# Five pairs of weight tiles in seven-product form in the input products of both feed-forward networks

## The reference

```python
D_MODEL, SEQ, D_FF = 2048, 256, 5504

def swiglu_ffn(x, w_in, w_out):
    gate, up = jnp.split(x @ w_in, 2, axis=-1)      # w_in: 2048 x 11008
    return (jax.nn.silu(gate) * up) @ w_out

x = x + 0.5 * swiglu_ffn(rmsnorm(x, ffn1_norm), ffn1_w_in, ffn1_w_out)
...
x = x + 0.5 * swiglu_ffn(rmsnorm(x, ffn2_norm), ffn2_w_in, ffn2_w_out)
```

## Time and profile before

| | us |
|---|---|
| median of 3 runs | 1764.4 (1764.1 to 1764.69) |
| the profiled execution, its own time | 1763.82 |
| its span, first to last instruction | 1762.0 |

### The profile page before, as it was taken

The page is one execution under the profiler, slowest core; times in us unless marked ns, Lnnn a source line. Parts: engine busy times, 40 slices in busy tenths (PEclk is TensorE's granted clock), DMA queues, the critical chain, the costliest instruction groups (busy, mean ns, idle before and its releaser), DMA issues.

```text
span 1762.0 us, 20916 instructions
## 1 busy us (share of the span) xinstructions
PE 1755.3 (100%) x8036; PEld 1463.3 (83%) x8036; DVE 1408.5 (80%) x1587; ACT 1074.9 (61%) x1359; POOL 62.7 (4%) x74
## 2 busy tenths in 40 slices
PE   9999999999999999999999999999999999999999
PEld 7788888888988888888888888888888888988887
DVE  7888888887899998575655655888888888799998
ACT  7566666666666666554545544666666666666665
POOL 0000000000000001100000000000000000000000
PEclk9999999999999999999999999999999999999999
DMA  9888788876654556555455547687788887764762
GB/s 378 272 261 260 251 250 249 252 252 201 217 215 184 210 215 208 178 193 177 160 188 163 173 168 262 169 256 244 249 260 260 260 261 240 226 204 166 259 213 90
DMA packets 160691, 391.75 MB, mean 222 GB/s; under 512 B 6504, under 2 KB 15232, under 8 KB 155856
## 3 DMA queue, kind: packets, MB, share of 16 engines
q1 hardware_dynamic: 152288, 342.02, 54.7%
q0 software_dynamic: 7184, 46.42, 12.6%
q10 hardware_dynamic: 1120, 1.97, 0.3%
HBM read 347.37 MB, written 3.69 MB: 199 GB/s over the span
## 4 chain that ended last, share of the span: by engine, by line
PE 95%; DVE 2%; DMA 1%; SPq 1%; issue 1%; ACT 0%; POOL 0%; ACTq 0%; POOLq 0%; DVEq 0%
PE bank L584 9%; PE bank L582 9%; PE bank L583 9%; PE bank L566 7%; PE bank L568 7%; PE bank L567 7%; PE bank L523 7%; PE bank L525 7%; PE bank L524 6%; PE bank L653 5%; PE bank L655 5%; PE bank L654 5%; PE bank L679 3%; PE bank L681 3%; PE bank L680 3%; PE bank L551 1%
## 5 line engine op out<-in xcount | busy, mean ns | idle before, releaser
L1188 DVE TENSOR_TENSOR wlo<-raw,whi 128x1024 fp32r<-128x1024 f32 (+1 forms) x586 | 696.6, 1207 | 224.7 <-ACT whi L849 222.0
L849 ACT ACTIVATE whi<-raw 128x1024 fp32r<-128x1024 f32 (+1 forms) x586 | 611.0, 1047 | 390.2 <-PE bank L525 189.2
L582 PE MATMUL bank<-whi,xs 128*128 128x512 f32 (+1 forms) x768 | 297.9, 388 | 0.4 <-DVE xs L1370 0.2
L584 PE MATMUL bank<-whi,xs 128*128 128x512 f32 (+1 forms) x768 | 295.6, 385 | 0.0
L583 PE MATMUL bank<-wlo,xs 128*128 128x512 f32 (+1 forms) x768 | 295.5, 385 | 0.0
L1188 DVE TENSOR_TENSOR wlo<-tsum,whi 128x1024 fp32r<-128x1024 f32 (+1 forms) x120 | 140.2, 1196 | 60.5 <-ACT whi L849 60.5
L849 ACT ACTIVATE whi<-tsum 128x1024 fp32r<-128x1024 f32 (+1 forms) x120 | 122.2, 1036 | 103.9 <-PE bank L584 64.1
L582 PEld LDWEIGHTS bank<-whi,xs 128*128 128x128 f32 x768 | 144.4, 188 | 29.0 <-issue 0.9
L584 PEld LDWEIGHTS bank<-whi,xs 128*128 128x128 f32 x768 | 144.3, 188 | 27.7
L583 PEld LDWEIGHTS bank<-wlo,xs 128*128 128x128 f32 x768 | 144.4, 188 | 26.8
L653 PE MATMUL bank<-whi,aw_hi 128*128 128x512 f32 x420 | 164.0, 391 | 0.0
(11 more groups left out here) (203 smaller groups left out, 2670.4 us busy)
## 6 DMA issues: line engine op xcount, KB each, us to landing
raw<-ffn_w_in SPq DMA_DIRECT2D x158, 1024.0 KB, 7.1
raw<-ffn_w_out SPq DMA_DIRECT2D x84, 1024.0 KB, 6.5
raw<-w_in SPq DMA_DIRECT2D x48, 1024.0 KB, 5.1
tsum<-raw POOLq DMA_DIRECT2D x36, 1024.0 KB, 7.2
raw<-w_out SPq DMA_DIRECT2D x16, 1024.0 KB, 4.9
raw<-ffn_w_in SPq DMA_DIRECT2D x16, 768.0 KB, 4.6
tsum<-raw POOLq DMA_DIRECT2D x4, 768.0 KB, 5.7
x<-x SPq DMA_DIRECT2D x4, 512.0 KB, 12.4
```

The lines of the kernel that those rows point to most:

```text
L582: mm(banks[b][:, 0:w], xs[:, k + i, 0, tok], hi, start=starts[b] and k + i == 0, stop=False, skip_group_check=True)
L584: last = mm(banks[b][:, 0:w], xs[:, k + i, 1, tok], hi, start=False, stop=k + i == last_k, skip_group_check=True)
L849: A(whi[:, h % SLOTS, 0:n_el], src, ACT.Copy).then_inc(weights_hi, 1)
L1188: V.tensor_tensor(wlo[:, h % SLOTS, 0:n_el], src, whi[:, h % SLOTS, 0:n_el].bitcast(f32), ALU.subtract).then_inc(weights_lo, 1)
```

## The change

The form now takes five pairs of tiles, k = 6 to 10 with k = 11 to 15. Each of the seven products has five tiles, in three halves of two, two and one tile ("mini" half, 512 numbers). The plain tiles are k = 0 to 5: three gate halves GA, GB, GC and three up halves UA, UB, UC. Raw pieces of five tiles go in two DMAs, four tiles into `raw` (five slots) and one into `minis`. The plain pieces are of two tiles, in three slots of their own. `minis`, `tmini` and `last_plain` take the place of `x` in SBUF during the units. So `x` is read again from DRAM behind each network's units (`x_again`), and ahead of the second network POOL first writes it there (`x_kept`). The ring of `whi` and `wlo` keeps four slots.

```diff
-T1, B11, G0, T2, B21, T3, G1, B22, T4, U0, U1 = 0, 2, 4, 6, 8, 10, 12, 14, 16, 18, 20
-UNIT_HALVES = 22
+FORM_K0, FORM_PAIRS = 6, 5
+T1, B11, GA, GB, T2, B21, T3, GC, B22, T4, UA, UB, UC = 0, 3, 6, 7, 8, 11, 14, 17, 18, 21, 24, 25, 26
+UNIT_HALVES = 27
...
+        place[0] = x_at
+        last_plain = sb("last_plain", [P, 2 * W])
+        minis = sb("minis", [P, FORM_SLOTS, W])
+        tmini = sb("tmini", [P, W])
...
             def form(h, bank_out, stationary, w, start):
-                for i in range(2):
+                for i in range(3):
                     pe.wait_ge(weights_lo, h + i + 1)
                     slot = (h + i) % SLOTS
-                    for k in range(2):
+                    for k in range(2 if i < 2 else 1):
...
+            def form_piece(u, j, name):
...
+                wait_free(n)
+                sp.dma_start(raw[:, raw_slot(n), 0:4 * w].rearrange("p (k f) -> p k f", k=4),
+                             w_in[:, k:k + 4, col:col + w]).then_inc(raw_full[raw_slot(n)], 16)
+                if j == 1 and name == "B11":
+                    sp.wait_ge(ss_done, 8 * (2 * u + 1))
+                    if u:
+                        sp.wait_ge(x_psum, 8)
+                        sp.wait_ge(x_stored, 16)
+                sp.dma_start(minis[:, raw_slot(n), 0:w], w_in[:, k + 4, col:col + w]).then_inc(raw_full[raw_slot(n)], 16)
...
             def add_piece(u, j, name, after, done):
...
+                pool.wait_ge(weights_lo, unit_half(u, j) + after + 3)
+                pool.wait_ge(raw_full[raw_slot(n)], RAW_FULL[n])
+                pool.dma_start(tsum[:, 0:4 * w], raw[:, raw_slot(n), 0:4 * w], accum_op=ALU.add).then_inc(done, 16)
+                pool.dma_start(tmini[:, 0:w], minis[:, raw_slot(n), 0:w], accum_op=ALU.add).then_inc(done, 16)
...
             x_power(2)
+            pool.wait_ge(x_updated, 8 * 2)
+            pool.dma_start(x_kept.rearrange("(b p) d -> p b d", p=P), x[:]).then_inc(x_stored, 16)
...
+                for i in range(3):
+                    form_split(T1, i)
+                form_split(B11, 0, "B11")
                 swiglu(u, j - 1)
-                split(base + B11 + 1, piece_half(n + LOAD["B11"], 1, w2), w2)
-                split(base + G0, piece_half(n + LOAD["G0"], 0, w2), w2)
-                split(base + G0 + 1, piece_half(n + LOAD["G0"], 1, w2), w2)
+                for i in range(1, 3):
+                    form_split(B11, i, "B11")
+                plain_split("GA", GA)
+                plain_split("GB", GB)
...
-                split(base + U0 + 1, piece_half(n + LOAD["U0"], 1, w2), w2)
-                split(base + U1, piece_half(n + LOAD["U1"], 0, w2), w2)
+                plain_split("UA", UA)
                 if j + 1 < UNITS:
                     sum_t1(u, j + 1)
-                split(base + U1 + 1, piece_half(n + LOAD["U1"], 1, w2), w2)
+                plain_split("UB", UB)
+                plain_split("UC", UC)
                 if j + 1 < UNITS:
                     sum_t3(u, j + 1)
```

More of the change, by code:

```diff
@@ L166, in sb @@
             return t
+        x_at = place[0]
         x = sb("x", [P, TB, D_MODEL])
+        x_end = place[0]
         xs_at = place[0]
@@ L362, in free, with wait_free @@
                 return weights_lo, QKV + 2 * (n - QKV_P) + 2
+            def wait_free(n):
+                slot = raw_slot(n)
+                shared = {RAW_SLOTS - 1: (RAW_SLOTS - 1, RAW_SLOTS, RAW_SLOTS + 1), RAW_SLOTS: (RAW_SLOTS - 1, RAW_SLOTS),
+                          RAW_SLOTS + 1: (RAW_SLOTS - 1, RAW_SLOTS + 1)}.get(slot, (slot,))
+                for t in shared:
+                    before = [m for m in range(n) if raw_slot(m) == t]
+                    if before:
+                        sem_free, value = free(before[-1])
+                        sp.wait_ge(sem_free, value)
@@ L995, in unit @@
-                act_e.wait_ge(weights_used, base + B11 + 2)
+                plain_split("GB", GB)
+                act_e.wait_ge(weights_used, base + B11 + 3)
                 act_e.wait_ge(act_f_done, 2 * (UNITS * u + j))
                 A(p1s[:, 0:w], Y[:, 0:w], ACT.Copy).then_inc(copied, 1)
-                act_e.wait_ge(t2_added, 16 * (first + 1))
-                for i in range(2):
-                    split(base + T2 + i, tsum[:, i * w2:(i + 1) * w2], w2)
-                loaded(n + LOAD["B21"])
@@ L1002, in unit @@
-                for i in range(2):
-                    split(base + B21 + i, piece_half(n + LOAD["B21"], i, w2), w2)
+                act_e.wait_ge(t2_added, 32 * (first + 1))
+                for i in range(3):
+                    form_split(T2, i)
+                loaded(unit_piece(u, j, "B21"))
+                for i in range(3):
+                    form_split(B21, i, "B21")
                 act_e.wait_ge(sums_done, 2 * first + 2)
-                split(base + T3, piece_half(n + LOAD["B12"], 0, w2), w2)
@@ L1006, in unit @@
-                act_e.wait_ge(weights_used, base + T2 + 2)
+                form_split(T3, 0, "B12")
+                act_e.wait_ge(weights_used, base + T2 + 3)
                 A(gset[:, s, 0, 0:w], Y[:, 0:w], ACT.Copy).then_inc(copied, 1)
-                split(base + T3 + 1, piece_half(n + LOAD["B12"], 1, w2), w2)
-                loaded(n + LOAD["G1"])
-                for i in range(2):
-                    split(base + G1 + i, piece_half(n + LOAD["G1"], i, w2), w2)
-                loaded(n + LOAD["B22"])
@@ L1023, in unit @@
-                split(base + U1, piece_half(n + LOAD["U1"], 0, w2), w2)
+                for i in range(1, 3):
+                    form_split(T3, i, "B12")
+                plain_split("GC", GC)
+                loaded(unit_piece(u, j, "B22"))
+                for i in range(3):
+                    form_split(B22, i, "B22")
+                act_copy(u, j - 1)
+                act_e.wait_ge(t4_added, 32 * (first + 1))
+                for i in range(3):
+                    form_split(T4, i)
+                plain_split("UA", UA)
@@ L1409, in unit, with form_split, plain_split @@
-                for i in range(2):
-                    split(base + G1 + i, piece_half(n + LOAD["G1"], i, w2), w2)
-                dve.wait_ge(weights_used, base + T3 + 2)
+                def form_split(form, i, name=None):
+                    src = form_half(unit_piece(u, j, name), i, w) if name else t_half(i, w)
+                    split(base + form + i, src, form_el(i, w))
+                def plain_split(name, half):
+                    split(base + half, plain_half(unit_piece(u, j, name), w2), w2)
@@ new lines, in unit @@
+                for i in range(3):
+                    form_split(T1, i)
+                form_split(B11, 0, "B11")
+                swiglu(u, j - 1)
+                for i in range(1, 3):
+                    form_split(B11, i, "B11")
+                plain_split("GA", GA)
+                plain_split("GB", GB)
+                for i in range(3):
+                    form_split(T2, i)
+                for i in range(3):
+                    form_split(B21, i, "B21")
+                for i in range(3):
+                    form_split(T3, i, "B12")
```

248 lines of the change are left out of this document (149 added, 99 removed).

## The result

| | before | after |
|---|---|---|
| median | 1764.25 (4 runs, 1763.71 to 1764.69) | 1812.11 (4 runs, 1810.03 to 1812.16) |
| the profiled execution: its time, its span | 1763.82, 1762.0 | 1812.06, 1810.3 |

The ratio is 1.0269, with an interval of 1.0251 to 1.0286: the changed kernel is **2.7% slower**, 48 us. The forecast was 1807, with a range of 1787 to 1828.

A forecast was written before the change was run, and what follows sets the result against it. PE was taken as the bound, busy 1755.3 of 1762.0 us. On 1763.82, -13.3 + 41.9 (both stalls) + 2.5 + 12 = +43.1 gave 1806.9, as a median 1807 us; range 1787 to 1828.

The forecast's parts named there:

- matmuls removed: PE's list in every unit: three matmuls fewer per unit, -13.3 us in all.
- stall A: PE waits at B11's second half, behind ring slot, DVE's split and `swiglu`: 1.10 us in 16 units, +21.6 in all.
- stall B: PE waits at UB because T1's sum stands ahead of its split on DVE: 1.2 us in 16 units, +20.3.
- first network's entry: Way into unit 1 of the first network: 2.9 us more DVE work ahead of T1, 0.4 to spare, +2.5 us.
- second network's entry: Way into unit 1 of the second network: loads wait for the store of `x`, +12 us, from 8 to 17.
- the walks: Step through a unit's operations with PE's and DVE's pitches, giving PE waits at B11's second half (1.10 us) and UB (1.2).
- The clock: Rival: PE's clock falls in the 12 us gap at the second network, T1's matmuls take 3.4 us more, 1810; chance 0.30.
- The store: POOL's 2 MB write of `x` to DRAM ahead of the second network's units, taken as 8 us.
- The late sums: Rival: POOL's sums by DMA for T2 land late, costing 1.1 us in each of 18 units, 1827; chance 0.10.
- DVE keeps up: Rival: no PE waits on DVE within units, and a short store, 1761.6 us, or 1753 with it hidden; chance 0.05.
- stall A alone: Rival: DVE is further ahead at UA, so only the wait at B11's second half comes, 1787 us; chance 0.12.

The follow-up runs named there:

- the best version: Variant with `swiglu` in two parts, plus POOL's 1.5 MB bias-vector copy moved behind the first network's units: 1754.69 us, ratio 0.9948 to the kernel before.
- all moves: Changed kernel with `swiglu` before B11's splits, T3's sums behind GB's split, T1's behind UB's, store before the power: 1764.32 us, ratio 0.9999.

## Why the prediction was right

The sum, term by term, against the profiled executions (a difference of 48.2):

| term | forecast | measured |
|---|---|---|
| matmuls removed | -13.3 | -13.3 (60 fewer) |
| stall A | +21.6 | +19.6: 1.05 in 16 units, 1.4 in two |
| stall B | +20.3 | +18.1: 1.08 in 16 units, 0.42 in two |
| slow matmuls behind each of these stalls | none | +5.4 |
| first network's entry | +2.5 | +3.4: gap 2.8, half clock 1.7, less the old wait, 1.1 |
| second network's entry | +12 | +13.4: gap 10.1, half clock 1.6, first T2 1.7 |
| the rest | 0 | +1.6 |
| sum | +43.1 | +48.2 |

- **The terms held.** Each of the two stalls came in the place and by the operations that the walks named, within 0.15 us of their size: 1.05 for 1.10 and 1.08 for 1.2. Only the 0.5 of stall A in each unit 1 isn't in this profile, where TensorE runs at half rate just ahead of it; in the variant with the store first, at full clock, PE waits 0.19 and 0.22 there. The transition from DVE to PE is 1.27, not the 1.37 of the earlier trace rows, which is most of the difference.
- **What the sum left out** is 5.4 us behind the stalls: a unit takes 43.49 where 41.02 and the two gaps make 43.15. The rows above show it: behind a wait of 0.92 the next matmul is 0.33 behind, and those that follow are at 0.23 and not at 0.227, at a granted clock of 1.00.
- **The nearness is in part luck.** The two stalls and the second entry's gap were put 6 us too high together. The slow matmuls, the clock, the late first T2 and the rest, of which the sum had nothing, came to 12, and the old wait that went gave 1.1 back. The first network's entry is this execution's own: in the six variants with the same code there the gap was 1.34 to 1.49 and the clock stayed full.
- **The clock**, a rival with a chance of 0.30, happened, and at the first entry too, where the forecast had not put it. It cost 1.6 us at the second, not 3.4, since about half of T1's matmuls ran at the lower rate; behind the same gap of some 10 us T1's 15 matmuls took 4.96 here and 5.19 to 6.27 in five variants, so up to 2.9 more than 3.40. The page "TensorE: Matmul & The Clock Gate" of the Trainium skill, section "What's actually happening", says that an idle PE is throttled to half speed; the granted 0.50 at 1155 agrees, while behind 3.28 us without work in the variant with `swiglu` in two parts the granted clock was 1.00.
- **The store** took 6.7 us where 8 was taken. The other estimate that the forecast gave beside it, from the Trainium skill's page "DMA: Bandwidth & Descriptors", section "Anatomy of one DMA", was 6.8, and was the better one; the gap is indeed 1.9 shorter than forecast.
- **The late sums**, rival three, did not come in the units (no POOL DMA ends a wait of PE there). They did at the first T2 of a network, 1.56 us in the second. ACT, at T1 + 10.8 in mid-network, waits for the small sum that was put at T1 + 10.1: 0.7 of the cover of 1.6 was gone, and stall A, which lies between, gave 1.05 back.
- **DVE keeps up** and **stall A alone** were wrong as 43.5 us a unit says.
- **What the reasons lacked** behind the right number. That stall A "needs no assumption on how far ahead DVE was" is so: with DVE 2.5 us early (T3's sum later) the stall was still 1.05. But it has a second cause that the forecast didn't name. DVE's queue was late by itself, to within 0.2 us of the ring (moving either one alone gave 1.4 and 0.3). The walks held this already: T1's splits, started at 17.1 with PE at 18.9, end 1.1 behind T1's first matmul, and the ring's slot comes at 1.3. Nor are the two stalls separate, at 20 each. Without stall B DVE would have been later still: its removal alone gave 5, where the forecast's rival priced its absence at 20. The stalls add up as a description of the trace, and not as the prices of two repairs. From 1812.1 they are taken out as 16.5 and 20.8, in one order, and as 5.2 and 32.2 in the other.

**Where the removed matmuls' gain went.** It was whole, 13.3 us, and 61.5 were added to it: a unit without waits takes 41.04 to 41.06, 0.66 below the 41.70 of before. In the best version the traces give 9.2 in all: 6.1 up to the second network's units, 5.0 in these, and -1.8 in the second network's out product, which takes 226.6 there and 224.8 before (first matmuls at 1523.05 and 1534.10, last at 1749.62 and 1758.85). That last term is in the changed kernel also, 226.1. It lies in matmuls that start some 0.1 to 0.4 late, now and then, in its first 90 us, and its cause was not sought.

## What to carry to other kernels

When work is added to an engine that feeds the bound one through a ring of slots, its share of busy time says little: walk through its list with pitches, and at every place write down both conditions, when the slot comes free and when the queue gets there. Where the two lie within a few tenths, an experiment that moves one of them alone shows nothing, and two such results without effect don't refute their sum; put everything between the due times into the places with room (here behind the plain gate halves), and test the moves together. And before a transfer is called slow, look what stands ahead of it in its queue that isn't due yet: a store behind a power operation cost 11 us here, a copy for a later stage 3 to 5.

## What was not expected of the hardware

- A wait of PE costs more than its length: behind gaps of some 1 us the first matmul comes 0.33 behind, the next nine at 0.23, together 0.15 us a gap, with the granted clock at 1.00 all the while.
- The granted clock was half after 2.65 and 9.93 us without work (T1's 15 matmuls took 5.09 in place of 3.40, then 4.96), and full after 1.34 to 1.60 us at the same two places in the variants. The length of the gap alone doesn't decide: at the first T2 it was full after 2.06 us (all moves) and after 3.28 (`swiglu` in two parts), longer than the 2.65 that brought the half clock. What else decides, no run here shows.
- A 256 KB DMA that adds onto SBUF, issued 0.6 us behind one of 1 MB of the same kind, has a median of 8.3 us from issue to landing in the changed kernel (6.1 to 11.4), more than the 6.9 of the larger one. The longest was at the second network's entry, where the loads are late; with the store first it took 8.9 there. At the first T2 it took up to 12.2 with the 1.5 MB copy ahead and 8.9 without.
